# RWKV layers of an encoder: the bonus products move from the end into the chunk loop

## The reference

```python
def rwkv7_mixer(h, w_in, mu, w0, w2, a0, a2, k_k, k_a, r_k, ln_g, ln_b, w_out):
    # r, k, v, g, decay, a: projections of h and of its shift, 16 heads of 64
    def step(S, inp):
        r_t, w_t, k_t, v_t, kk_t, b_t = inp
        sa = jnp.einsum('bhvk,bhk->bhv', S, -kk_t)
        S = S * w_t[:, :, None, :] + sa[..., None] * b_t[:, :, None, :] + v_t[..., None] * k_t[:, :, None, :]
        return S, jnp.einsum('bhvk,bhk->bhv', S, r_t)
    _, y = lax.scan(step, S0, xs)
    y = jnp.moveaxis(y, 0, 1)
    y = head_norm(y, ln_g, ln_b, RW_GN_EPS)
    y = y + jnp.sum(r * k * r_k.astype(F32), axis=-1, keepdims=True) * v
    y = y.reshape(B, T, RW_WIDTH) * jax.nn.silu(g.astype(F32))
    return y.astype(h.dtype) @ w_out
```

## Time and profile before

| | us |
|---|---|
| median of 3 runs | 1420.39 |
| lowest and highest | 1418.88, 1421.83 |
| the profiled execution | 1421.91 |
| its span, from the first to the last instruction | 1420.1 |
| TensorE busy | 1330.4 (94%) |
| VectorE busy | 721.1 (51%) |
| ScalarE busy | 406.1 (29%) |
| GpSimd busy | 97.5 (7%) |

### The profile page before, as it was taken

The page is one execution under the profiler, slowest core; times in us unless marked ns, Lnnn a source line. Parts: engine busy times, 40 slices in busy tenths (PEclk is TensorE's granted clock), DMA queues, the critical chain, the costliest instruction groups (busy, mean ns, idle before and its releaser), DMA issues. The chain is left out here.

```text
span 1420.1 us, 23223 instructions
## 1 busy us (share of the span) xinstructions
PE 1330.4 (94%) x10019; PEld 686.4 (48%) x10019; DVE 721.1 (51%) x1390; ACT 406.1 (29%) x916; POOL 97.5 (7%) x118
## 2 busy tenths in 40 slices
PE   5999999999898999889899998999899999999997
PEld 3443444488444444564434445544343444468633
DVE  5686776965532011361345013532686875975552
ACT  1124364055201020560112052501021367135401
POOL 0000251010100000000000000000000054011100
PEclk9999999999999999999999999999899999999999
DMA  6221222100600222101222221122322222200411
GB/s 215 75 74 47 72 75 61 30 5 5 240 0 15 75 84 78 45 5 57 76 60 79 82 61 30 36 69 74 126 74 62 57 73 63 59 3 4 149 49 59
DMA packets 111181, 92.43 MB, mean 65 GB/s; under 512 B 5020, under 2 KB 99524, under 8 KB 110568
## 3 DMA queue, kind: packets, MB, share of 16 engines
q1 hardware_dynamic: 110376, 88.82, 20.5%
q10 hardware_dynamic: 704, 2.13, 0.4%
HBM read 84.65 MB, written 6.29 MB: 64 GB/s over the span
## 5 line engine op out<-in xcount | busy, mean ns | idle before, releaser
L1017 PE MATMUL bank<-arena 128*128 128x512 f32 x960 | 420.3, 595 | 1.5 <-ACT arena L601 1.5
L965 PE MATMUL bank<-arena 64*64 64x64 f32 (+6 forms) x6848 | 318.5, 247 | 22.4 <-issue 10.4
L1017 PEld LDWEIGHTS bank<-arena 128*128 128x128 f32 x960 | 179.9, 190 | 227.7 <-issue 216.3
L965 PEld LDWEIGHTS bank<-arena 64*64 64x64 f32 (+3 forms) x6848 | 203.9, 133 | 147.6 <-issue 127.5
L159 ACT ACTIVATE arena<-arena 128x1024 f32<-128x1024 f32 x20 | 21.1, 1056 | 233.7 <-DVE arena L951 122.0
L726 DVE SCALAR_TENSOR_TENSOR arena<-arena 128x512 f32<-128x512 f32 x96 | 73.3, 809 | 0.0
L1714 PE MATMUL bank<-arena 128*128 128x512 f32 x160 | 71.1, 605 | 1.6 <-PEq L301 1.6
L627 ACT ACTIVATE arena<-arena 32x128 f32<-32x128 f32 x128 | 54.4, 425 | 37.0 <-DVE arena L748 34.3
L542 POOL MEMSET arena<- 128x8 f32 x2 | 0.2, 113 | 911.9 <-DVE arena L879 911.9
L1346 PE MATMUL bank<-arena 128*128 128x512 f32 x128 | 55.2, 593 | 1.6 <-PEq L510 1.6
L2123 PE MATMUL bank<-arena 128*128 128x512 f32 x128 | 55.8, 593 | 0.9 <-DVE arena L2167 0.9
(11 more groups left out here) (225 smaller groups left out, 1504.0 us busy)
## 6 DMA issues: line engine op xcount, KB each, us to landing
arena<-in_rw_w_in SPq DMA_DIRECT2D x66, 512.0 KB, 4.1
arena<-in_ml_w_in SPq DMA_DIRECT2D x24, 512.0 KB, 3.9
arena<-in_sw_w_in SPq DMA_DIRECT2D x20, 512.0 KB, 3.8
arena<-in_rw_w_out SPq DMA_DIRECT2D x16, 512.0 KB, 7.1
spill<-arena SPq DMA_DIRECT2D x2, 2048.0 KB, 8.9
arena<-spill SPq DMA_DIRECT2D x2, 2048.0 KB, 14.7
arena<-in_sw_w_out SPq DMA_DIRECT2D x8, 512.0 KB, 3.5
arena<-in_ml_w_out SPq DMA_DIRECT2D x8, 512.0 KB, 3.6
```

Source lines behind the costliest of these rows:

```text
L965: mm = lambda out, a, b, start=True, stop=True: nc.tensor.matmul(out, a, b, start=start, stop=stop, skip_group_check=True)
L1017: last = nc.tensor.matmul(bank[:, :], slot[:, k, :], mix_at[what][:, k, :], start=k == 0, stop=k == KT - 1)
```

## The change

The bonus products 0 to 6 move into the chunk loop: bonus(c) stands between state_outputs(c) and products_r(c+1). All of them use bank 1, one after another, and VectorE multiplies each with the values and writes the result into R, between place_transpose(c+1) and mask_r(c+1). ScalarE's three copies and GpSimd's three products are gone. bonus(7) stands behind the first spreads, its product with the values behind finish(1). To have bank 1 free, the transposed keys of chunks 1 to 6 use banks 0 and 2; with this banks_23_read waits for their copies too, and turn_bk waits for two readers of bank 2 before its second half. The first spreads, now three, stand directly behind the second sums; each later one stands alone behind the products of one k. The banks of the output products are dealt out anew, and SP loads the final gain into V's place.

```diff
-RW_OUT_BANKS = ((1, 2, 3, 7), (0, 4, 5, 6))
+RW_OUT_BANKS = ((2, 3, 6, 7), (4, 5, 0, 1))
-BY_VALUES = 5
-    t_bank = lambda c, q: m.bank[q if c else 6 + q]
+    t_bank = lambda c, q: m.bank[2 * q if c else 6 + q]
-    fg = m.view(B_R, D)
+    fg = m.view(B_V, D)
-    spread_bank = lambda j: m.bank[(4, 5, 0, 6)[j % 4]]
-    bonus_bank = lambda j: m.bank[(1, 2, 3, 6, 7)[j % 5]]
+    spread_bank = lambda j: m.bank[(4, 5, 0)[j % 3]]
+    bonus_bank = m.bank[1]
...
-                sp.wait_ge(bonus_done.handle, bonus_done.at(KT))
+                sp.wait_ge(bonus_used.handle, bonus_used.at(KT))
...
-            for j in range(BY_VALUES, KT):
-                pool.wait_ge(bonus_kept.handle, bonus_kept.at(j - BY_VALUES + 1))
-                nc.gpsimd.tensor_tensor(R[:, j, :], R[:, j, :], V[:, j, :], ALU.mult).then_inc(bonus_times_v.handle, 1)
...
-            for j in range(BY_VALUES, KT):
-                act.wait_ge(bonus_done.handle, bonus_done.at(j + 1))
-                nc.scalar.activation(R[:, j, :], bonus_bank(j)[:, :], ACT.Copy).then_inc(bonus_kept.handle, 1)
...
+            def times_values(j):
+                dve.wait_ge(bonus_done.handle, bonus_done.at(j + 1))
+                nc.vector.tensor_tensor(R[:, j, :], bonus_bank[:, :], V[:, j, :], ALU.mult).then_inc(bonus_used.handle, 1)
...
                     keep_x(c + 1)
                     place_transpose(c + 1)
+                    times_values(c)
                     mask_r(c + 1)
...
             invert_roots(0, 0, SUMMED)
-            for j in range(3):
-                times_values(j)
             invert_roots(1, SUMMED, T)
-            for j in range(3, BY_VALUES):
-                times_values(j)
             for j in range(KT):
                 finish(j)
+                if j == 1:
+                    times_values(KT - 1)
...
                 pe.wait_ge(gr_evac.handle, gr_evac.at(2 * given["r"]))
+                pe.wait_ge(bkt_evac.handle, bkt_evac.at(2 * given["turned"]))
...
             def turn_bk(c):
                 if c > 0:
-                    banks_01_read()
+                    pe.wait_ge(v_evac.handle, v_evac.at(given["values"]))
...
                 for q in range(2):
+                    if c > 0 and q == 1:
+                        pe.wait_ge(gr_evac.handle, gr_evac.at(2 * c + 1))
+                        pe.wait_ge(xs_ready.handle, xs_ready.at(c + 1))
...
                 state_outputs(c)
                 if c + 1 < NC:
+                    bonus(c)
                     products_r(c + 1)
-                else:
-                    bonus(0)
-                    bonus(1)
                 outputs(c)
...
-            bonus(2)
             sums(1, SUMMED, T)
-            for j in range(3, KT):
-                bonus(j)
-            spread(range(4))
+            spread(range(3))
+            bonus(KT - 1)
             for k in range(KT):
...
-                if k in (1, 3):
-                    spread(range(k + 3, k + 5))
+                if k + 3 < KT:
+                    spread((k + 3,))
```

More of the change, by code:

```diff
@@ L504, in rw_layer @@
         "eps_set", "y_squared", "last_y_squared", "sums_done", "root_ready", "rstd_ready", "pick_loaded", "h_reloaded"))
-    bonus_done, bonus_used, bonus_kept, bonus_times_v, spread_done, spread_used, finished, out_done = (m.sem(n) for n in (
-        "bonus_done", "bonus_used", "bonus_kept", "bonus_times_v", "spread_done", "spread_used", "y_finished", "out_done"))
+    bonus_done, bonus_used, spread_done, spread_used, finished, out_done = (m.sem(n) for n in (
+        "bonus_done", "bonus_used", "spread_done", "spread_used", "y_finished", "out_done"))
     w_loaded = [m.sem(f"w_out{k}_loaded") for k in range(KT)]
@@ L918, in invert_roots @@
                 nc.vector.reciprocal(rstd[:, at:to], rstd[:, at:to]).then_inc(inverse.handle, 1)
-            def times_values(j):
-                dve.wait_ge(bonus_done.handle, bonus_done.at(j + 1))
-                nc.vector.tensor_tensor(V[:, j, :], bonus_bank(j)[:, :], V[:, j, :], ALU.mult).then_inc(bonus_used.handle, 1)
             def finish(j):
@@ L928, in finish @@
                     .then_inc(spread_used.handle, 1)
-                if j < BY_VALUES:
-                    dve.wait_ge(bonus_used.handle, bonus_used.at(j + 1))
-                else:
-                    dve.wait_ge(bonus_times_v.handle, bonus_times_v.at(j - BY_VALUES + 1))
+                dve.wait_ge(bonus_used.handle, bonus_used.at(j + 1))
                 dve.wait_ge(spread_used.handle, spread_used.at(j + 1))
                 link(nc.vector.scalar_tensor_tensor(out=KK[:, j, :], in0=KK[:, j, :], scalar=col(RW_LNB, j),
-                                                    in1=(V if j < BY_VALUES else R)[:, j, :], op0=ALU.add, op1=ALU.add))
+                                                    in1=R[:, j, :], op0=ALU.add, op1=ALU.add))
                 nc.vector.tensor_tensor(KK[:, j, :], KK[:, j, :], G[:, j, :], ALU.mult).then_inc(finished.handle, 1)
             invert_roots(0, 0, SUMMED)
-            for j in range(3):
-                times_values(j)
             invert_roots(1, SUMMED, T)
-            for j in range(3, BY_VALUES):
-                times_values(j)
             for j in range(KT):
                 finish(j)
+                if j == 1:
+                    times_values(KT - 1)
             def add(dve, n):
@@ L1036, in _, with bank_0_read @@
             given = {"values": 0, "x": 0, "xu": 0, "r": 0, "turned": 0}
-            def banks_01_read():
+            def bank_0_read():
                 pe.wait_ge(v_evac.handle, v_evac.at(given["values"]))
@@ L1084, in turn_values @@
             def turn_values(c):
-                banks_01_read()
+                bank_0_read()
                 for p in range(KT):
@@ L1185, in bonus @@
                     pe.wait_ge(scaled_rk.handle, scaled_rk.at(NC))
[L1186 to L1191, removed]
+                else:
+                    pe.wait_ge(bonus_used.handle, bonus_used.at(j))
+                mm(bonus_bank[:, :], bones, R[:, j, :]).then_inc(bonus_done.handle, 1)
             def spread(js):
                 for j in js:
-                    if j >= 4:
-                        pe.wait_ge(spread_used.handle, spread_used.at(j - 3))
+                    if j >= 3:
+                        pe.wait_ge(spread_used.handle, spread_used.at(j - 2))
                     elif j == 0:
@@ L1200, in spread @@
                         pe.wait_ge(y_evac.handle, y_evac.at(2 * NC))
-                    elif j == 3:
-                        pe.wait_ge(bonus_used.handle, bonus_used.at(4))
                 for j in js:
@@ L1258, in _ @@
                 for a in range(NT):
[L1259 to L1263, removed]
                     last = out_product(0, a, k)
@@ L1281, in rw_layer @@
                  (u_cleared, BC), (s_cleared, 1), (scaled_rk, NC), (x_done, NC), (xs_ready, NC), (xu_done, NC), (us_ready, NC), (u_placed, NC), (eps_set, 1), (y_squared, NC - 1), (last_squared, 2), (sums_done, 2), (root, 2),
-                 (inverse, 2), (pick_loaded, 64), (reloaded, 16), (bonus_done, KT), (bonus_used, BY_VALUES), (bonus_kept, KT - BY_VALUES),
-                 (bonus_times_v, KT - BY_VALUES), (spread_done, KT), (spread_used, KT), (finished, KT), (out_done, 8), (added, 8),
+                 (inverse, 2), (pick_loaded, 64), (reloaded, 16), (bonus_done, KT), (bonus_used, KT),
+                 (spread_done, KT), (spread_used, KT), (finished, KT), (out_done, 8), (added, 8),
                  (rhs_begun, NC), (v_done, NC), (v_evac, NC), (rhs_done, NC), (sa_done, NC)):
```

## The result

| | before | after |
|---|---|---|
| median, us | 1419.64 (4 runs) | 1435.60 (4 runs) |
| ratio | 1 | 1.0097, 95% interval 1.008 to 1.0114 |
| the profiled execution, us | 1421.91 | 1434.39 |
| its span, us | 1420.1 | 1432.6 |
| TensorE busy, us | 1330.4 | 1342.9 |

A forecast was written before the change was run, and what follows sets the result against it. TensorE was taken to be full in loop and output products, waiting only in the tail. Terms summed to +8.6 us per layer, +17.2 for both, added to the median 1420.39: 1437.6 us, range 1429 to 1446.

The forecast's parts named there:

- a loop of about 88 us: Sign that the forecast is right: the chunk loop grows by some 11 us, from 76.3 to about 88.
- Tail, -5.6 a layer: After the last chunk: outputs, sums and first spreads start earlier and finish(0) is quicker, -5.6 us per layer.
- Bonus products, +8.2 a layer: Chunk loop: seven bonus products at 1.17 us each all lie on TensorE's path, +8.2 us; times_values is hidden.
- Wait before xu, +5.4 a layer: Chunk loop: xu waits for copies of turned keys, 0.9 us in each of 6 chunks, +5.4 us per layer.
- rival 5: The clock falls inside the loop, each fall costing up to 3 us; two make 1443.6; chance 0.08.
- Instruction standstills, -2.2 a layer: Chunk loop: bonus products give instruction fetches time where they fall between packet and standstill, -2.2 us (0 to -4.8).
- Spreads, +3.8 a layer: Output products: single spreads make 3 more pieces at 1.25 us each, a pair costing as much as one; +3.8 us.
- Clock, -1.0 a layer: Behind the tail: shorter standstills recover part of the 2.6 us lost at the lower clock, -1.0 us (-2.7 to +0.5).
- a loop that hides all: Rival 1: the loop hides bonus products and wait, leaving only tail, spreads and clock; -5.6 us, 1414.8; chance 0.04.

The follow-up runs named there:

- its later run: The changed kernel, unaltered, run once more beside its variants, against the kernel before; 1.0105, 1437.01 us.
- the wait alone: Kernel before with one edit: banks_23_read also waits for ScalarE's copies of the turned keys, which stay in banks 0 and 1; 1.012, 1438.26 us.

## Why the prediction was right, and which terms were off

**Direction and size.** The forecast was +17.2 us; 14 to 16 were measured. The argument that the change removes no work from TensorE, adds a wait and switches and recovers only the tail held. That the loop is full held in part only: it took in some 6 us of products a layer without growing longer. The stated sign of a loop of about 88 us was missed, with 85.1, one fall of the clock included.

**Tail, -5.6 a layer.** Right, piece by piece: 12.95 became 7.35 in the second layer, with the slow second step of finish(0) at 0.75. In the table of stretches the tail moved 371 GB/s and TensorE still waited for engines alone, so no transfer had come in place of the wait.

**Bonus products, +8.2 a layer.** The price of one was right (1.17 forecast, 1.15 from the chunks). times_values was hidden: no wait of TensorE for L817 appears in the loop.

**Wait before xu, +5.4 a layer.** Right in place, number and size (0.90). What the sum left out is its effect on the clock, which stood only as rival 5: one fall in the profiled loops of the changed kernel, none in its later run, and three in the run with the wait alone. The range's upper half had this.

**Instruction standstills, -2.2 a layer.** The term that was mis-sized. About 6 us a layer were paid back, more than the 4.1 to 5.4 of issue time which I had taken for the most there could be. Two errors: I took only the pauses that the view of waits names as the amount, though the chunks also ran slower between them (9.3 to 11.3 us long for the same work); and I held that a bonus product helps only a standstill close behind it, while in fact nearly all of them vanished. The runs with one long and sixteen short products show that long work in this place is paid back and short work is not. That what decides is the time a chunk gives the fetch per instruction is argued and not shown, and the wait alone, with its issue time intact, speaks against it as the whole rule; I have no explanation that a run supports. The pause lies in another place of the chunk than the long product, and a long product was not tried there.

The Trainium skill (Runtime: NRT & Kernel Launch, Instruction fetch mechanics) holds that fetching the next block is hidden behind issue. The traces speak against it here: 4.1 to 5.9 us of issue time per loop wherever the matmuls are all short, each standstill ending 2.2 to 2.9 us behind the start of a packet, and none in the kernel before with one long product added.

**Spreads, +3.8 a layer.** Right: +3.9 in the second layer, and taken back by grouping. In the first it shows as +2.0, the clock's earlier fall having taken the rest.

**Clock, -1.0 a layer.** Wrong. The longest standstill in the tail shrank from 2.97 to 1.35 and the clock fell all the same, from 1359.3 in the table above, as from 1350.2. I had argued from the longest gap; around the fall stood four gaps, of 0.73, 0.48, 1.02 and 1.35 us, and TensorE had 3.85 us of work in the 7.3 us of the tail. What of this brought the fall no run shows.

So the size came out partly by luck, as two errors went opposite ways: 4 us a layer too much, for what was paid back, and 1 us a layer too little for the clock in the tail and about 1.5 for each of its other falls. The changed kernel's profile has two such, at 1270.5 and, in the attention layer's first products, at 451.3. Together 17.2 - 8 + 2 + 3 = 14.2. The second of these falls stands in every variant of the changed kernel and not in the kernel before or its three variants; its cause is open.

The rival on the other side, a loop that hides all, was 0.04. Its first half came closer than I gave it credit for: most of the bonus products' time was hidden, but in the time that the loop lost and not behind the wait for sa, which the rival had named. With the bank kept, the change would have measured as no difference, and with the spreads kept too as a gain of 0.5%.

## What to carry to other kernels

When work moves into a loop that seems full, ask what kind of full: compare the longest with the shortest turn of the same loop, since that difference, and not only the named waits, is what the added work may be paid from, if the work is long for its number of instructions. Ask then for the semaphores that come with it: here a buffer moved by one bank cost 11 to 14 us, and seven bonus products in each layer 5.4 to 6.1. Small matmuls that run side by side in different row groups should be issued together, and if a tail has several short waits, each can hold a piece of independent work, which may save the clock too: it did in one layer of two.

## What the runs showed of the hardware that was not expected

- One product of 128x512 (1.15 us) in each of 14 chunks made the time 1.0013 of before (0.9996 to 1.003); sixteen of 32x32 (some 0.7 us) in the same place made it 1.007 (1.0047 to 1.0094).
- The 15 standstills of TensorE called issue in the two loops of the kernel before, 0.2 to 1.5 us each, all end 2.3 to 2.9 us after a 16 KB packet of the instruction queue starts.
- Cut into eight of 64 columns, a 128x512 product took about 0.9 us longer: a pass of 128x64 followed the last after 0.11 us, more than an eighth of the 0.43 us of 128x512.
- TensorE's granted clock was 0.51 (the lower level, 1.2 GHz) from 1296.3 to 1303.0 inside a loop, after a wait of 0.83 us and, 2 us later, a standstill of 1.25 us. In the kernel before a standstill of 1.13 us stood alone, and the clock stayed at 1.00.
